# Pair decays of the mixing stage from stored running sums: broadcast matmuls of 64 rows and a rectifier before the exponential

## The reference, cut to what matters

```
gc = jnp.cumsum(blocks(g), axis=-1)
decay = jnp.exp(jnp.where(causal, gc[..., :, None] - gc[..., None, :], -jnp.inf))
L = jnp.where(strict, jnp.einsum('nbhcd,nbhjd->nbhcj', kb, kc) * decay, 0.0)
qk = jnp.einsum('nbhcd,nbhjd->nbhcj', qc, kc) * decay
```

## Time and profile before

| what | value |
|---|---|
| time of the kernel, median of 3 runs | 2378.61 us (2376.11 to 2386.3) |
| the profiled execution's own time | 2375.67 us |
| span of its trace | 2373.8 us |
| mean granted TensorE clock | 0.953 |
| TensorE busy | 2207.2 us, 93% |
| VectorE busy | 1277.0 us, 54% |
| ScalarE busy | 543.2 us, 23% |
| GpSimd busy | 641.0 us, 27% |

### The profile page before, as it was taken

How to read it: one execution, slowest core, us unless ns; L and a number is a source line. 1 busy time by engine, 2 the same in 40 slices (tenths; PEclk the granted TensorE clock), 3 DMA queues, 4 the chain that set the end, 5 groups by cost and what they waited for, 6 DMA issues and landing times. The chain is left out here.

```text
span 2373.8 us, 47036 instructions
## 1 busy us (share of the span) xinstructions
PE 2207.2 (93%) x18536; PEld 1200.9 (51%) x18536; DVE 1277.0 (54%) x2659; ACT 543.2 (23%) x1417; POOL 641.0 (27%) x819
## 2 busy tenths in 40 slices
PE   7999999999975999898999999857999999999977
PEld 4454454454444666665666666633444444444433
DVE  4515325233424565355675756546776667667746
ACT  3202103112112344233434334310000000000013
POOL 1020100100200110211132231316655555555452
PEclk9999999999986899899999999977999999999998
DMA  8041040130168031112311221147999999999967
GB/s 311 22 136 45 24 142 23 47 112 13 33 177 224 11 114 53 52 57 73 119 65 63 92 92 62 44 159 274 346 372 362 370 373 367 379 376 370 351 224 311
DMA packets 171951, 405.87 MB, mean 171 GB/s; under 512 B 51187, under 2 KB 92771, under 8 KB 147161
## 3 DMA queue, kind: packets, MB, share of 16 engines
q1 hardware_dynamic: 142423, 350.39, 41.5%
q0 software_dynamic: 23648, 35.19, 4.1%
q10 hardware_dynamic: 5698, 17.67, 1.9%
HBM read 344.98 MB, written 94.80 MB: 185 GB/s over the span
## 5 line engine op out<-in xcount | busy, mean ns | idle before, releaser
L876 PE MATMUL p_ps<-p_xt,p_w 128*128 128x512 f32 x1088 | 474.1, 594 | 0.5 <-DVE p_xt L697 0.5
L3075 PE MATMUL p_ps<-p_w_arena,p_x_arena 128*128 128x512 f32 x1024 | 452.3, 595 | 11.1 <-DVE p_x_arena L2977 11.1
L876 PEld LDWEIGHTS p_ps<-p_xt,p_w 128*128 128x128 f32 x1088 | 204.1, 190 | 253.7 <-issue 248.5
L3075 PEld LDWEIGHTS p_ps<-p_w_arena,p_x_arena 128*128 128x128 f32 x1024 | 195.4, 191 | 257.2 <-issue 246.0
L2731 POOL DMA_INDIRECT p_x_arena<-s_hn,p_slot x272 | 275.9, 1014 | 122.2 <-issue 63.4
L2371 PE MATMUL p_ps<-p_w_out,p_mixt 128*128 128x512 f32 x544 | 254.7, 612 | 0.2 <-DVE p_mixt L1977 0.2
L2999 DVE STREAM_TRANSPOSE p_y_arena<-p_y_arena 32x64 f32<-32x64 f32 x1024 | 240.9, 235 | 13.2
L3084 PE MATMUL p_ps<-p_w_arena,p_y_arena 128*128 128x512 f32 x512 | 230.2, 592 | 3.2 <-DVE p_y_arena L2999 3.2
L3084 PEld LDWEIGHTS p_ps<-p_w_arena,p_y_arena 128*128 128x128 f32 x512 | 97.2, 190 | 126.0 <-issue 126.0
L2371 PEld LDWEIGHTS p_ps<-p_w_out,p_mixt 128*128 128x128 f32 x544 | 100.4, 194 | 105.1 <-issue 101.8
L885 PE MATMUL p_ps<-p_w,p_xt 128*128 128x144 f32 (+1 forms) x512 | 146.6, 439 | 0.0
(11 more groups left out here) (419 smaller groups left out, 2840.1 us busy)
## 6 DMA issues: line engine op xcount, KB each, us to landing
p_w_arena<-in_w_exp_gate SPq DMA_DIRECT2D x64, 1024.0 KB, 12.1
p_w_arena<-in_w_exp_up SPq DMA_DIRECT2D x64, 1024.0 KB, 14.4
p_w_arena<-in_w_exp_down SPq DMA_DIRECT2D x64, 1024.0 KB, 9.2
p_w_arena<-s_y SPq DMA_DIRECT2D x16, 1024.0 KB, 14.8
p_x<-in_x_prompt SPq DMA_DIRECT2D x30, 512.0 KB, 3.5
p_w<-in_w_in SPq DMA_DIRECT2D x4, 2048.0 KB, 14.5
p_spread<-s_roots SPq DMA_DIRECT2D x16, 512.0 KB, 7.0
s_kv<-p_us SPq DMA_DIRECT2D x32, 256.0 KB, 2.6
```

Of the source, the lines that this page charges most:

```text
L876: ins = mm(ps[:, job % 4, :], w[:, c, at:at + P], xt[s % 2][:, c, :], start=(c == 0), stop=(c == KC - 1))
L3075: t = mm(ps[:, 2 + b, :], xt[b][:, c, :], w_gu[bw][:, :, c, :], start=(c == 0), stop=(c == KC - 1))
```

## The change

Running sums replace the masked product. The transposed running sums of all prompt tiles are made once before the loop and kept as `g_rows`, 128 x 128: partition n*64 + 4*tile + k holds head k of half n, along it the 128 tokens. The sums with tokens on partitions are kept as `g_sum`. For a prompt tile, `pair_sums` spreads one row of `g_rows` over all partitions by a matmul with 64 rows: the stationary operand is one column of the identity, broadcast to 128 columns. There are eight of these of 64 x 128 by 64 x 128, alternating between the two halves of the array and between banks 2 and 3. ScalarE then computes `relu(g_sum - spread)` per head, which bounds the pairs in the wrong order at zero, and in a second pass the exponential of its negative with the bias of before. The sample tile keeps the old way (GpSimd's product once, two full matmuls), in banks 2 and 3.

`pair_sums(t + 2)` moves on TensorE from the tail to behind `new_values(t, 2)`. `key_products` takes over the wait for `dec_ready`, since it writes the banks that the decays are read from; the waits for `dec_ready` in `scores` and `logits` are gone. Per tile GpSimd's product goes. The identity moves from the list `SECOND` to `FIRST`. A fourth and a fifth sum, two copies on VectorE and one on GpSimd are added before the loop, and `pair_decays(1)` comes before `far_copy(0)`.

```diff
             def pair_decays(t):
-                qkt_ready.after(act, t - 1)
+                dsum_done.after(act, t)
+                qk_read.after(act, t - 1)
                 lt_ready.after(act, t - 1)
-                for n in two:
-                    dsum_done.after(act, t, n + 1)
-                    for k in range(4):
-                        ins = nc.scalar.activation(dec[:, 4 * n + k, :], ps[:, 6 + n, k * P:(k + 1) * P], ACT.Exp,
-                                                   bias=gates[:, data(t), 2 * H + 4 * n + k:2 * H + 4 * n + k + 1])
+                src, bias, scale = ps[:, 2:4, :].rearrange("p a (h t) -> p (a h) t", h=4), gates[:, data(t), 2 * H:], 1.0
+                if t != SI:
+                    for k in range(H):
+                        ins = nc.scalar.activation(dec[:, k, :], src[:, k, :], ACT.Relu, bias=g_sum[:, data(t), k:k + 1], scale=-1.0)
+                    ins.then_inc(limited.sem, 1)
+                    limited.after(act, t)
+                    src, scale = dec, -1.0
+                for k in range(H):
+                    ins = nc.scalar.activation(dec[:, k, :], src[:, k, :], ACT.Exp, bias=bias[:, k:k + 1], scale=scale)
                 ins.then_inc(dec_ready.sem, 1)
...
             def pair_sums(t):
-                gt_ready.after(pe, t)
-                for n in two:
-                    mm(ps[:, 6 + n, :], (s_after if t == SI else after)[:], gt[:, 4 * n:4 * n + 4, :].rearrange("p h t -> p (h t)"),
-                       start=True, stop=True).then_inc(dsum_done.sem, 1)
+                qk_read.after(pe, t - 1)
+                lt_ready.after(pe, t - 1)
...
+                for k in range(4):
+                    for n in two:
+                        row = n * HD + 4 * data(t) + k
+                        ins = mm(ps[:, 2 + n, k * P:(k + 1) * P], ident[half_of(n), row:row + 1].to_broadcast([HD, P]),
+                                 g_rows[half_of(n), :], start=True, stop=True)
+                ins.then_inc(dsum_done.sem, 1)
 
             def key_products(t):
                 b = t % 2
                 pe.wait_ge(kq_in[b], use(t))
                 invt_ready.after(pe, t - 1)
+                dec_ready.after(pe, t)
...
-            for n, m in enumerate((upto, after, ones)):
-                ins = mm(ps[:, n % 2, n * NT * H:(n + 1) * NT * H].rearrange("p (t h) -> p t h", t=NT), m[:],
-                         gates[:, 0:NT, 0:H], start=True, stop=True)
+            for bank, m in ((0, upto), (1, after), (5, ones), (6, upto)):
+                ins = mm(ps[:, bank, 0:NT * H].rearrange("p (t h) -> p t h", t=NT), m[:], gates[:, 0:NT, 0:H],
+                         start=True, stop=True)
             ins.then_inc(on["gates_done"], 1)
+            pe.wait_ge(on["g_cols_ready"], 1)
+            mm(ps[:, 4, 0:P], g_cols[:].rearrange("p n t k -> p (n t k)"), upto[:], start=True, stop=True
+               ).then_inc(on["g_rows_done"], 1)
+            pe.wait_ge(on["g_rows_ready"], 1)
+            pair_sums(0)
             pe.wait_ge(on["e_ready"], 3)
-            pair_sums(0)
             key_products(0)
...
                 new_values(t, 2)
+                if t + 2 < NQ:
+                    pair_sums(t + 2)
...
-                if t + 2 < NQ:
-                    if back:
-                        h_ready.after(pe, t - 1)
-                    swa_mixed.after(pe, t)
-                    pair_sums(t + 2)
```

More of the change, by code:

```diff
@@ L2281, in scores @@
                     pe.wait_ge(ak_in[b], use(t))
-                    dec_ready.after(pe, min(t + 1, NQ - 1))
                     lg_ready.after(pe, t - 2)
@@ L2417, in _ @@
             far_products(0)
-            dec_ready.after(pe, 0)
-            pair_sums(1)
             far_update(0)
```

50 lines of the change are left out of this document (30 added, 20 removed).

## The result

| kernel | median | range, runs | ratio |
|---|---|---|---|
| before | 2379.1 us | 2368.11 to 2386.3, 10 | 1 |
| changed | 2401.01 us | 2394.07 to 2419.55, 10 | 1.0109 (95%: 1.0086 to 1.0133) |

The changed kernel is slower by 22 us by the medians, and the interval of the ratio leaves out 1. So the two traces stand 31 us apart, not 22, and that matters when terms are compared.

What follows compares the result with a forecast made beforehand. TensorE was taken to bound the kernel, busy 42.24 of 43.00 us a prompt tile. Middle 13.3, sample tile 1.0, tail 0, start 2.8 and clock 8.5 gave +25.6 on 2375.67: 2401 us, own range 2390 to 2412, 80% range 2381 to 2418.

Steps and rivals of the forecast that it cites:

- Bound: Middle of a tile: TensorE waits for nobody, so added sums cost in full, 0.95 us a tile, +13.3 over 14.
- Tail: End of a tile: ScalarE's sixteen activations hold up logits, so it gives back 0.1 us at most, taken as 0.
- Before the loop: Start: identity, transposed sums and later key_products, partly regained at tile 1's sums: +2.8 us, ends -2 and +6.
- Clock: Tails with idle times lose the granted clock: five of 14 at 1.7 us each, +8.5; range 0 to 24.
- The tail gives back all: Rival: TensorE's timeline shrinks by the full 1.95 us a tile in the tail, 2362 us, faster; chance 0.10.
- Half given back: Rival: the tail gives back half and no clock is lost, 2382 to 2387 us, no measurable change; chance 0.20.
- The halves don't pair: Rival: the new 64-row matmuls in the middle don't pair, +13 more, 2414 us; 0.17 together with the clock rival.
- The clock falls in each tail: Rival: every tail loses the clock, +15 more, 2416 us; chance 0.17 together with halves not pairing.
- The rectifier needs another activation table: Rival: two table loads a tile in ScalarE's tail, +36 more, 2437 us; chance 0.03.

Runs made afterwards that it cites:

- e12: e1 with the eight matmuls of the sums ordered four of the lower 64 rows, then four of the upper, not alternating: 2401.5 us, ratio to before 1.0126.
- e1: The changed kernel with ScalarE's sixteen activations for tile t+2 issued ahead of the square of h, no longer behind it: 2386.1 us, ratio to before 1.0027.
- e2: The changed kernel with the bound at zero of tiles 2 to 16 computed by VectorE, not ScalarE's rectifier: 2389.3 us, ratio to before 1.0053.
- e3: The changed kernel plus two unread full matmuls a tile, ahead of turn_hn and of logits: 2388.2 us, ratio to before 1.0036.
- e11: The changed kernel with sums in the tail, activations behind ScalarE's tail copies, the logits copy between rectifiers and exponentials, key_products behind scores 1: 2363.8 us, ratio to before 0.9950.
- e8: The changed kernel with the sums in two halves in the tail, ScalarE's sixteen activations behind its tail copies: 2379.4 us, ratio to before 1.0045.
- e6: The changed kernel with the old product, two full matmuls and eight exponentials for tiles 2 to 16, matmuls in the middle: 2452.6 us, ratio to before 1.0344.

## Why the prediction was right, and where it wasn't

The median came out at 2401.0, where 2401 was predicted. The steps did less well than the sum. I added 25.6 to the profiled execution of before, which lay 3.4 below the median of ten runs; measured are 22 by the medians and 26 by the ratio.

**Bound.** Right: the middle pays each microsecond. At 1.09 from start to start the sixteen records bring 15.3 over 14 tiles. I had 0.95 and 13.3, so this term was 2.0 short; the twin rows were a fair guide, and half the columns of `key_products` at equal pairing was a little too kind. e12 shows that matmuls that take turns overlap. The price of the Trainium skill's "TensorE: Matmul & The Clock Gate", section "Back-to-back issue gap", 81 ns a matmul of 128 columns, would have made it 1.3, an estimate by that page; the row says 0.068 us a record. The measurement lies between the two, a little nearer to 0.95.

**Tail.** Right, nearly to the row. I gave idle times of 0.5, 0.5 and 0.9; in most tiles they are 0.52, 0.44 and 0.84 to 1.1. From `level_products` 3 to `logits` the usual tile takes 5.12 from start to start, 5.29 before, so it gives back 0.17, where I had 0.1 at most. Over all fifteen tails it comes to nothing, as I took it, for a few are longer: in the shown tile the waits are 0.67, 0.96 and 1.11. There VectorE waits 0.42 us for GpSimd's root, a link that I had left out, and so it does in six of the seventeen tiles. The rectifiers took 2.15 as predicted; the exponentials from SBUF start every 0.29 to 0.30, and I had 0.28. e1 and e2 confirm which engine ends the last wait: either one takes it away.

**Before the loop.** +2.8 predicted, +1.0 measured (first `state_products` at 754.36, 753.35 before). The first `key_products` came at 719.36, and I had said 719.8, so that start was right. It ended at 723.15 and not at 722.1, since at half speed it takes 3.79 and not 2.29. What made up for it was the stretch from its end to `state_products`: 36.2 us before, 31.2 now. I had 2.2 of these 5.0. The rest is about what fell away of idle times that the profile puts down to "issue", inside the lines of 32x32 matmuls: 11.8 us in that stretch before, 8.8 now.

**Clock.** The term that was mis-sized. I took five tails that lose 1.7 us each, 8.5. The number of tails was about right: the clock falls at eleven of fifteen, where it fell at five before, so six more. The length was not: I took 3.4 us at half speed for each, and the eleven last 10 us on the mean. In the whole loop, from the first `state_products` to the last, 165 us are at half speed and 99 before; 8 of them are the first of the loop, because the clock that was low before the loop came back at 762.1 and not at 753.0. 66 more at 0.41 are 27 us (an estimate), by the runs it is (283 - 228) x 0.41 = 23. e3 shows that the tail's idle time is the cause of the greater part.

**What offset it.** 15.3 + 1.0 + 0 + 1.0 + 27 = 44, and 22 were measured, 31 between the two traces. Two things that I had taken for fixed were not. The chain of waits on TensorE over the loop, the kernel before:

```profile
PE p_ps L2143 <- DMA p_kq<-s_kq: 6.9, 1, 6.9
PE p_ps L2184 <- issue: 5.9, 4, 2.4
...
PE p_ps L2195 <- issue: 1.8, 1, 1.8
```

and the changed one (microseconds in total, times, longest):

```profile
PE p_ps L2400 <- DVE p_hn L1998: 10.9, 13, 2.9
PE p_ps L2408 <- issue: 9.6, 12, 1.1
...
PE p_ps L2164 <- DMA p_kq<-s_kq: 3.7, 2, 3.5
```

The wait of `key_products` for its keys fell from 6.9 to 3.7, because a slower loop comes later to the same transfer; in e1_decays_first, which is faster than the changed kernel, it is 11.2 again. And the stalls in `far_products` and `far_update` (L2184, L2195), 7.7 us together, have only 1.0 to set against them in the changed kernel's loop (two in L2194). That is 10 us, and it brings 44 to 34, near the 31 of the traces; the other 3 are not accounted for. The medians' 22 is 9 less because the profiled execution of the changed kernel lay above its median and that of before below. So the number was right by luck: a clock term three times too small, no term for waits that a slower loop covers nor for stalls that come and go, and a base that was 3.4 low.

What the stalls are, "issue" doesn't say, but the DMA records give a strong hint. Each of the five of before ends 2.3 to 2.7 us after the start of a transfer of 16 KB on the queue that the profile's page calls "q8 instruction". In the thirteen traces TensorE has 61 such stalls of over 0.8 us in this stage (the waits of `logits` and `key_products`, which ScalarE ends, left out), and 59 of them end 2.2 to 2.9 us after such a start; stretches of that kind cover 11% of the time. It looks as if TensorE waited there for its own instructions. That is inferred, and no run was aimed at it; why a stall falls in one kernel and not in the next stays open.

**Rivals.** "The tail gives back all" is out by the rows of the tail; in e11 a time like the one that I gave there, faster than before, comes true by other orders on TensorE and ScalarE. "Half given back" is out. "The halves don't pair" is out by e12, where matmuls of one half and one bank in a row take half as long again. "The clock falls in each tail" came closest: the clock's term is as large as I gave it there (15 more), though only with the offset it ends at 2401. No table load stands in the loop, so that "The rectifier needs another activation table" is out; the Trainium skill, "ScalarE: Activation LUTs", section "Table sets: the hidden batching unit", has relu in every set, and the trace agrees.

## What to carry to other kernels

Work taken off a busy engine pays only if what the others deliver is early enough; here ScalarE's copy was ready 0.1 us ahead of `logits` and `hn` 1.1 ahead of its transposes, and what was added to ScalarE's line in the tail came back on TensorE with the clock on top. Before work moves, list for each engine the idle time that stands next to a wait of another one: ScalarE had 6.4 us free ahead of the square, and one swapped pair of calls was worth 15 to 20 us, as much as the sums cost in the middle. And a change of operations should be measured in its own best place, and so should what it replaces: the same eight matmuls and sixteen activations gave 2436, 2401, 2378 and 2364 us. The old operations had a bad place too (2453, and 2397 with one instruction of GpSimd moved).

## What the runs showed of the hardware

- 64-row float32 matmuls of 128 columns with a stationary operand that is one column broadcast: 1.09 us for 8 (16 records) if row halves and PSUM banks alternate, 1.64 if both do only once (e12), 1.30 in two groups of four (e8).
- ScalarE from PSUM and from SBUF: eight rectifiers of 128 columns last 2.15 to 2.18, eight exponentials from SBUF 2.45 (e1). Eight of VectorE's two-step operations from PSUM take 2.16 (e2).
- VectorE's operation with two inputs from SBUF lasts 1.28 us alone. Beside a GpSimd product of 1.9 that started first it lasts 1.28 plus the overlap less 0.2, up to 2.91, and the product keeps its length (e6, thirteen tiles).
- Adding 2.4 us of useless matmuls a tile to a kernel bound by TensorE made it 13 us faster, and the granted clock rose from 0.941 to 0.954 (e3). Between runs of the changed kernel each microsecond at 1.2 GHz goes with 0.41 us, between those of before with 0.47.
- The clock fell at eleven of fifteen tails whose single idle times are mostly 0.4 to 1.1 us, and stayed at 1.2 GHz for 10 us on the mean. With two of the three waits filled (e3) it fell at three of fifteen, and with the last one gone (e1, in a profiled execution that was one of its fastest) at three or four.
- Of TensorE's 61 stalls of over 0.8 us that are put down to "issue" and that no other engine explains, 59 end 2.2 to 2.9 us after the start of a 16 KB transfer on the instruction queue (thirteen traces).
